# Layer-norm sums taken from nearly finished tiles, summed mLSTM strips, single-pass selector rows, three output units at the last heads, and four output transfers

## The reference: what is computed

```python
def layer_norm(x, g, b):
    xf = x.astype(jnp.float32)
    mu = jnp.mean(xf, axis=-1, keepdims=True)
    var = jnp.mean(jnp.square(xf - mu), axis=-1, keepdims=True)
    return ((xf - mu) * lax.rsqrt(var + LN_EPS)).astype(x.dtype) * g + b
...
    b = jnp.cumsum(lf, axis=-1)
    dmat = jnp.where(causal, b[..., :, None] - b[..., None, :] + ig[..., None, :], -jnp.inf)
...
    sm = w_intra * jnp.einsum('bhtd,bhsd->bhts', q, k)
    num = jnp.einsum('bhts,bhsv->bhtv', sm, v) + w_inter[..., None] * jnp.einsum('bhtd,bhdv->bhtv', q, C)
    den = jnp.sum(sm, axis=-1) + w_inter * jnp.einsum('bhtd,bhd->bht', q, n)
    h = num / jnp.maximum(jnp.abs(den), jnp.exp(-m_t))[..., None]
...
    h = h * lax.rsqrt(jnp.mean(h * h, axis=-1, keepdims=True) + RMS_EPS)
    return (h * jax.nn.sigmoid(o_pre)) @ w_out
```

## Time and profile before

| what | value |
|---|---|
| median of 3 runs | 2621.55 us (2618.34 to 2622.1) |
| the profiled execution | 2622.95 us |
| its span | 2620.9 us |
| outside the span | 2.05 us |
| PE busy | 95% of the span |
| granted TensorE clock, mean | 0.964 |

### The profile page before, as it was taken

The page is one execution under the profiler, slowest core; times in us unless marked ns, Lnnn a source line. Parts: engine busy times, 40 slices in busy tenths (PEclk is TensorE's granted clock), DMA queues, the critical chain, the costliest instruction groups (busy, mean ns, idle before and its releaser), DMA issues.

```text
span 2620.9 us, 33849 instructions
## 1 busy us (share of the span) xinstructions
PE 2480.9 (95%) x11937; PEld 2007.9 (77%) x11937; DVE 1488.6 (57%) x1796; ACT 499.2 (19%) x968; POOL 1647.5 (63%) x700
## 2 busy tenths in 40 slices
PE   6998999998999997999999999999999999999997
PEld 4776776776888875888888878888887667888886
DVE  5867324686464467755444465534688456544446
ACT  4533221103000004111111230000141442100000
POOL 4425544575777774756665657777777224787774
PEclk7999999998999997999999999999999888999998
DMA  6212333422332322222222223323322111232331
GB/s 241 74 54 85 114 148 128 157 73 66 96 104 86 102 87 67 85 77 77 83 78 84 77 76 96 109 77 98 108 82 81 41 33 49 92 104 84 96 106 54
DMA packets 61231, 237.72 MB, mean 91 GB/s; under 512 B 7072, under 2 KB 12200, under 8 KB 57424
## 3 DMA queue, kind: packets, MB, share of 16 engines
q1 hardware_dynamic: 54720, 230.51, 26.8%
q10 hardware_dynamic: 6416, 5.95, 0.7%
HBM read 232.24 MB, written 2.10 MB: 89 GB/s over the span
## 4 chain that ended last, share of the span: by engine, by line
PE 84%; DVE 8%; ACT 2%; issue 2%; DVEq 1%; ACTq 1%; DMA 1%; POOL 1%; POOLq 0%
PE gg L559 19%; PE gg L560 19%; PE gg L561 19%; PE babcd L597 2%; PE babcd L599 2%; PE babcd L598 2%; PE gg L934 2%; PE gg L936 1%; PE gg L935 1%; PE babcd L559 1%; PE babcd L560 1%; PE babcd L561 1%; PE babcd L1179 1%; PE be L910 1%; PE be L1205 1%
## 5 line engine op out<-in xcount | busy, mean ns | idle before, releaser
L467 POOL TENSOR_TENSOR w_hi<-raw,zero 128x1024 fp32r<-128x1024 f32 (+2 forms) x260 | 540.5, 2079 | 453.1 <-PE gg L561 348.2
L469 POOL TENSOR_TENSOR w_lo<-raw,w_hi 128x1024 fp32r<-128x1024 f32 (+2 forms) x260 | 695.3, 2674 | 37.7 <-issue 1.3
L559 PE MATMUL gg<-h_hi,w_hi 128*128 128x512 f32 x1560 | 621.0, 398 | 8.9 <-DVE bf L2349 4.9
L560 PE MATMUL gg<-h_lo,w_hi 128*128 128x512 f32 x1560 | 615.7, 395 | 0.0
L561 PE MATMUL gg<-h_hi,w_lo 128*128 128x512 f32 x1560 | 615.0, 394 | 0.0
L559 PEld LDWEIGHTS gg<-h_hi,w_hi 128*128 128x128 f32 x1560 | 298.2, 191 | 80.2 <-DVE bf L2349 7.2
L458 POOL TENSOR_TENSOR w_hi<-raw,zero 128x1024 fp32r<-128x1024 f32 (+2 forms) x64 | 139.8, 2184 | 332.1 <-PE babcd L561 153.7
L561 PEld LDWEIGHTS gg<-h_hi,w_lo 128*128 128x128 f32 x1560 | 297.8, 191 | 63.2
L560 PEld LDWEIGHTS gg<-h_lo,w_hi 128*128 128x128 f32 x1560 | 298.4, 191 | 61.3
L2059 DVE TENSOR_TENSOR ta<-ff_s,gg 128x512 f32<-128x512 f32 x63 | 43.4, 688 | 320.3 <-PE gg L561 320.3
L559 PE MATMUL gg<-u_hi,w_hi 128*128 128x512 f32 x528 | 209.7, 397 | 4.2 <-issue 4.2
(11 more groups left out here) (601 smaller groups left out, 3916.7 us busy)
## 6 DMA issues: line engine op xcount, KB each, us to landing
raw<-in_w_ff_in_a SPq DMA_DIRECT2D x66, 512.0 KB, 3.5
raw<-in_w_ff_in_b SPq DMA_DIRECT2D x66, 512.0 KB, 3.5
raw<-in_w_att_qk SPq DMA_DIRECT2D x48, 512.0 KB, 3.5
raw<-in_w_ff_out_a SPq DMA_DIRECT2D x24, 704.0 KB, 4.1
raw<-in_w_ff_out_b SPq DMA_DIRECT2D x24, 704.0 KB, 4.1
late_raw<-in_w_ada SPq DMA_DIRECT2D x16, 1024.0 KB, 5.0
raw<-in_w_ml SPq DMA_DIRECT2D x25, 512.0 KB, 3.5
raw<-in_w_merge_a SPq DMA_DIRECT2D x16, 768.0 KB, 5.6
```

The source lines that it names most:

```text
L467: pool.tensor_tensor(hi, a, zero[:].to_broadcast([P, size * P]), ALU.add)
L469: pool.tensor_tensor(lo, a, hi, ALU.subtract).then_inc(S["units_split"], 1)
L559: pe.matmul(dst, w_hi[slot][:, blk], xs[0][:, k, :], start=k == 0, stop=False)
L560: pe.matmul(dst, w_hi[slot][:, blk], xs[1][:, k, :], start=False, stop=False)
```

## The change

LN0 and LN1: tile 7 is no longer added to `ta` and `tb`. PE column-sums `ta` and `tb` of tiles 0 to 6 as soon as they are ready, then tile 7 and its square, and makes the row sums last, in two float32 matmuls. Centring and scaling are done tile by tile, and POOL makes `h_lo` (`low_tiles`), behind its third split. Attention: three blocks of unit 0 stand ahead of head 7's scores, and the third unit is done inside the last head, in a bank of its own. mLSTM projections: `gate_sums` moves from conv 3 to conv 1, `gate_columns` from conv 5 to conv 4, `gate_turn` from ahead of conv unit 7 to behind it; a new `gate_rows` after conv 2 splits the gate rows into rounded and rest parts (fp32r, partitions 0 to 7 and 32 to 39), so that a selector on 40 partitions spreads a row in a single pass. ACT loads that selector five times over and rounds it. Heads: the rows of head i+1 stand behind head i's values, score block 2 stands inside the gate unit after its fourth block, and the denominator takes two matmuls (128 and 384 wide) in place of four, from `sm_sum`, which DVE adds up in three instructions. `last_heads` takes the third output unit in. End: the last square is summed by PE alone, and four transfers of 512 KB from two queues, each as soon as its two tiles are ready.

```diff
+            def low_tiles(stage):
+
+                for k in range(KD):
+                    pool.wait_ge(S["h_high"], H_SPLIT[stage] - 7 + k)
+                    pool.tensor_tensor(h_lo[:, k, :], (ta, tb)[k % 2][:], h_hi[:, k, :], ALU.subtract).then_inc(S["h_split"], 1)
...
+                        if s == 2 and name in ("w_ff0_in_a", "w_att"):
+                            low_tiles("ff0" if name == "w_ff0_in_a" else "att")
...
                 pe.wait_ge(S["x_summed"], nth + 1)
-                pe.matmul(bf[:], ones[:], ta[:], start=True, stop=True).then_inc(S["ln_rows"], 1)
-                for n, a in enumerate((ta, tb)):
-                    for b in range(TB):
-                        mm = pe.matmul(be[:, n * TB + b:n * TB + b + 1], a[:, b * P:(b + 1) * P], ones[:, 0:1], start=True, stop=True)
-                mm.then_inc(S["ln_sum"], 1)
+                sums(0, ta, start=True)
+                sums(1, tb)
+                pe.wait_ge(S["ln_centred"], nth * 8 + 8)
+                sums(0, last)
+                pe.wait_ge(S["sq_ready"], (SQ["ln0"], SQ["ln1"])[nth] * 8 + 8)
+                sums(1, sq[1], stop=True).then_inc(S["ln_sum"], 1)
+                pe.matmul(bf[:], ones[:], ta[:], start=True, stop=False)
+                pe.matmul(bf[:], ones[:], last, start=False, stop=True).then_inc(S["ln_rows"], 1)
...
-                    for s in range(2):
+                    for s in range(int(lead is not None and isinstance(i, int)), 2):
...
-                        third = lead is not None and isinstance(i, int) and s == 0
-                        cols_mm(g[(u0 + s) % 2], THIRD[name] if third else (u0 + s) % 2, kb, xs, **(first if isinstance(i, int) and s == 0 else {}))
+                        cols_mm(g[(u0 + s) % 2], (u0 + s) % 2, kb, xs, **(first if isinstance(i, int) and s == 0 else {}))
...
+                    bank, slot = ((g[u0 % 2], u0 % 2), (g[(u0 + 1) % 2], (u0 + 1) % 2), (bf[:], THIRD["w_att_out"]))[s]
...
+                        tile_mm(bank, slot, k, (o_hi, o_lo))
                 pe.wait_ge(S["att_copied"], 48)
+                unit(0, 0, 3)
                 att_scores(7, 1)
-                unit(0, 0, 7)
+                unit(0, 3, 7)
                 att_swap(7)
                 unit(1, 0, 7)
                 att_turn(7)
+                unit(2, 0, 4)
                 att_values(7, 1)
-                unit(0, 7, 8)
-                unit(1, 7, 8)
+                unit(2, 4, 7)
+                for s in range(3):
+                    unit(s, 7, 8)
...
                     pe.wait_ge(S["ml_w"], i)
-                    pe.wait_ge(S["ml_sm"], 4 * i)
-                pe.matmul(ba if i else be[:], sel8[:, i, :], g_r[:], start=True, stop=True)
-                pe.matmul(bb if i else bf[:], sel8[:, i, :], g_m[:], start=True, stop=True).then_inc(S["ml_rows"], 1)
+                    pe.wait_ge(S["ml_sm"], 5 * i - 1)
+                pe.matmul(ba if i else be[:], sel[:, i, :], g_r2[:], start=True, stop=True)
+                pe.matmul(bb if i else bf[:], sel[:, i, :], g_m2[:], start=True, stop=True).then_inc(S["ml_rows"], 1)
...
-                wait(pe, "ml_sm", 4 * i)
+                wait(pe, "ml_sm", 5 * i)
                 if i == 0:
                     pe.wait_ge(S["conv_in"], 8)
-                for j in (0, 1, 3, 2):
-                    if j == 2:
+                def block(j):
+                    return pe.matmul(score_bank(i, j), ml_qk[rows, it + 4, j * P:(j + 1) * P], ml_qk[rows, it, j * P:SEQ],
+                                     start=True, stop=True)
+                for j in (0, 1, 3):
+                    block(j)
+                def third_block(k):
+                    if k == 4:
                         pe.wait_ge(S["ml_em"], i + 1)
-                    mm = pe.matmul(score_bank(i, j), ml_qk[rows, it + 4, j * P:(j + 1) * P], ml_qk[rows, it, j * P:SEQ],
-                                   start=True, stop=True)
-                mm.then_inc(S["ml_scores"], 1)
...
-                    pe.wait_ge(S["ml_sm"], 4 * i + j + 1 if i else 4)
+                    pe.wait_ge(S["ml_sm"], 5 * i + j + 1 if i else 4)
                     part = sm_t[:, ML_AT[j]:ML_AT[j] + SEQ - j * P]
                     pe.matmul(be[:, j * P:SEQ], ml_v[:, j, i * P:(i + 1) * P], part, start=j == 0, stop=j == 3)
-                    mm = pe.matmul(bf[:, j * P:SEQ], ones[:], part, start=j == 0, stop=j == 3)
-                mm.then_inc(S["ml_num"], 1)
+            def head_sums(i):
+
+                pe.wait_ge(S["ml_sm"], 5 * i + 5)
+                pe.matmul(bf[:, 0:P], ones[:], sm_t[:, 0:P], start=True, stop=True)
+                pe.matmul(bf[:, P:SEQ], ones[:], sm_sum[:], start=True, stop=True).then_inc(S["ml_num"], 1)
...
                 conv_unit(n)
+                if n == 7:
+                    gate_turn()
                 value_unit(n - 1)
                 if n == 2:
                     pe.wait_ge(S["gates_read"], 1)
                     inverse_columns(5, bf)
-                if n == 6:
-                    gate_turn()
             head_rows(0)
             value_unit(7)
             for i in range(8):
-                if i:
-                    head_rows(i)
-                head_scores(i)
-                output_gate(i)
+                output_gate(i, head_scores(i))
                 if i > 1:
                     norm_rows(i - 2)
                 head_values(i)
                 if i:
                     square_sums(i - 1)
+                if i < 7:
+                    head_rows(i + 1)
+                head_sums(i)
...
+                    bank, slot = ((g[u0 % 2], u0 % 2), (g[(u0 + 1) % 2], (u0 + 1) % 2), (be[:], THIRD["w_ml_out"]))[s]
+                    if first == 0:
+                        ready(u0 + s)
...
+                        tile_mm(bank, slot, k, (hd_hi, hd_lo), H_SPLIT["head"] - 8)
...
+                unit(2, 0, 2)
                 norm_rows(7)
+                unit(2, 2, 6)
                 for k in (6, 7):
-                    for s in range(2):
+                    for s in range(3):
                         unit(s, k, k + 1)
...
+            for a, name, value in ((tb, "sq_added", nth * 8 + 7), (sq[1], "sq_ready", nth * 8 + 8)):
+                pe.wait_ge(S[name], value)
+                for b in range(TB):
+                    mm = pe.matmul(be[:, b:b + 1], a[:, b * P:(b + 1) * P], ones[:, 0:1], start=a is tb and b == 0,
+                                   stop=a is not tb and b == TB - 1, skip_group_check=True)
+            mm.then_inc(S["sq_summed"], 1)
...
+            act.activation(sel[:], sel_in8[:], ACT.Copy)
...
+            for k in (0, 4):
+                act.wait_ge(S["out_ready"], k + 2)
+                act.dma_start(out[:, k:k + 2, :], x[:, k:k + 2, :]).then_inc(S["out_sent"], 16)
+            act.wait_ge(S["out_sent"], 64)
...
+                    third = {"w_att_out": bf[:], "w_ml_out": be[:]}.get(name)
+                    bank = third if third is not None and k == 2 else g[(u0 + s) % 2]
...
+                        if k == KD - 1:
+                            return
...
+                        if k == KD - 2:
+                            v.drain().then_inc(S["x_summed"], 1)
...
+                if squares != SQ["final"]:
+                    add_square(squares, KD - 1)
...
-                centre(4, KD)
-                v.drain()
-                wait(v, "rows_ready", nth + 1)
-                make(0)
-                make(1)
+                wait(v, "ln_rows", nth + 1)
                 for k in range(KD):
-                    wait(v, "h_high", H_SPLIT[stage] - 7 + k)
-                    v.tensor_tensor(h_lo[:, k, :], (ta, tb)[k % 2][:], h_hi[:, k, :], ALU.subtract).then_inc(S["h_split"], 1)
-                    if k + 2 < KD:
-                        make(k + 2)
+                    v.scalar_tensor_tensor(x[:, k, :], bf[:], -1.0 / D, x[:, k, :], ALU.mult, ALU.add)
+                    v.drain()
+                    if k == 0:
+                        wait(v, "rows_ready", nth + 1)
+                    make(k)
                 v.drain()
...
+            def gate_rows():
+                for whole_row, two in ((g_r, g_r2), (g_m, g_m2)):
+                    v.memset(two[:].bitcast(F32), 0.0)
+                    v.drain()
+                    v.tensor_copy(two[0:8, :], whole_row[:])
+                    v.drain()
+                    v.tensor_tensor(two[32:40, :], whole_row[:], two[0:8, :], ALU.subtract)
+                v.drain()
...
-                if n == 3:
+                if n == 1:
                     gate_sums()
-                if n == 5:
+                if n == 2:
+                    gate_rows()
+                if n == 4:
                     gate_columns()
...
+                v.drain()
+                own = lambda j: sm_t[:, ML_AT[j]:ML_AT[j] + SEQ - j * P]
+                tt(sm_sum[:], own(0)[:, P:SEQ], own(1), ALU.add)
+                tt(sm_sum[:, P:3 * P], sm_sum[:, P:3 * P], own(2), ALU.add)
```

(2 more changed lines are left out.)

73 lines of the change are left out of this document (40 added, 33 removed).

## The result

The changed kernel takes 2615.78 us (median of 13 runs, 2610.35 to 2619.85) against 2620.48 of the kernel before on the same chips (13 runs, 2615.69 to 2624.63): a ratio of 0.998, 95% interval 0.9971 to 0.999. It is faster by 4.7 us, which is near what can be told from no change, and not by the 49 that were forecast. The profiled execution has a span of 2616.8 us.

The account below looks back on a forecast made before the run. PE, busy 95% of the span, was taken as the bound; terms of −9.8 −0.4 −8.2 −25.8 −2.3 −2.6 = −49.1 us gave a span of 2571.8 and a median of 2572.5, range 2564 to 2582 (chance 0.50).

Parts of the forecast that it names:

- The loop that is: mLSTM heads: PE no longer bounds; a chain over additions, `og`, tanh, |den| and products takes 15.4 us a head.
- a clock above 0.9 in the heads: Sign to look for in the changed kernel's profile: PE's granted clock in the mLSTM heads, 0.84 before.
- 1.1 us a head: mLSTM heads: the first addition waits for the end of POOL's second split instruction, +1.1 us in each head.
- Rival (d): mLSTM heads: each of three additions waits for a whole POOL instruction, up to 7 us a head; chance 0.02.
- Rival (a): mLSTM heads: the clock falls as often as before, about 9 to 12 us more, 2583; chance 0.20.
- a loop of 13.2 on DVE and ACT: mLSTM heads: the forecast's sum for one head's chain without the three additions, 13.2 us.
- its 25.8: mLSTM heads: the gain forecast for seven heads, 103.3 us against 129.1.
- Layer norms: LN0 and LN1: additions gone and tiles scaled sooner, gains of 4.6 and 5.2 us, together −9.8.
- the case that I had named for −14: LN0 and LN1: outer bound of the gain, if the clock stays up through the sums.
- Third units: Last heads: filling PE's gaps gives −0.4 us in attention, −2.3 in mLSTM, as POOL's next split holds PE up.
- Projections: mLSTM projections: earlier gate work and single-pass rows gain, `gate_rows` costs PE 2.1 us; together −8.2 us.
- End: Kernel end: column sums replace the last add, +0.25 us; four 512 KB transfers, 3.5 us each, save 2.8; together −2.6.

Follow-up runs that it names:

- low_last: Changed kernel with `hd_lo` moved on DVE behind `og` and the two products of `head_norm`; 2604.86 us, ratio 0.9943.
- old_order_sums: old_heads with the strip additions and two denominator matmuls put back, right behind the value matmuls; 2594.51 us, ratio 0.9905.
- old_heads: four_strips with rows at a head's start and score block 2 ahead of the gate unit, as before the change; 2591.16 us, ratio 0.989.
- pool_waits: Changed kernel with POOL's split in the heads, and for the first two `w_ml_out` units, waiting for the gate copy; 2595.25 us, ratio 0.9902.
- sums_first: Changed kernel with denominator ahead of square sums and rows, `hd_lo` behind `og` and `head_norm`, POOL's split waiting for the `og` copy; 2586.36 us, ratio 0.9878.
- four_strips: Changed kernel without the strip additions, the denominator in four matmuls again; 2578.72 us, ratio 0.985.

## Why the prediction was wrong

**The step that failed** is the sum of "The loop that is" for the heads: 15.4 us a head, 103.3 for seven; measured are 19.6 and 137.4. That is 34 of the 45 us by which the span is off (2571.8 against 2616.8). The sum lacks a path and has a wait too small, and the clock, which it takes as high, fell with them. The loops, from windows of each trace:

| run | loop | PE idle in it | mean clock |
|---|---|---|---|
| before | 129.4 | 0.0 | 0.84 |
| changed kernel | 137.4 | 11.6 | 0.78 |
| low_last | 130.8 | 15.2 | 0.86 |
| old_order_sums | 126.9 | 14.5 | 0.81 |
| old_heads | 119.2 | 8.3 | 0.90 |
| pool_waits | 118.7 | 10.3 | 0.91 |
| sums_first | 105.6 | 9.0 | 0.98 |
| four_strips | 103.5 | 0.3 | 0.98 |

A mean clock of 0.78 over 137.4 us is some 30 us lost, in pool_waits at 0.91 some 11, so most of what was paid was paid at the lower clock and not in the waits themselves. The forecast asked for a clock above 0.9 in the heads.

First, the path. I let the loop run over `og`, tanh and |den|, with the denominator's matmuls free to go when the additions were done. But they stand on PE behind the square sums and the next rows, and the square sums wait for `og` (`og_copied`, in `square_sums`), which stands on DVE behind the additions and `hd_lo`. So the additions and this order of PE delay everything on it. pool_waits shows this without waits for POOL: its loop is 15.2 us longer than that of four_strips, about 2 in a plain cycle (16.96 against 14.73 to 15.0) and most of it in the two that have half clock. Of the 15.2, sums_first takes back 13.1 with the additions kept, by the denominator ahead of the square sums and `hd_lo` behind `og`, which were not tried apart. It is the order that cost, more than the additions themselves.

Second, place and size of the waits for POOL. I had 1.1 us a head, for the first addition, behind a split that starts ahead of the products. In the changed kernel the split starts behind the first addition in seven of eight heads, and the wait was up to 2.0 for the second, 2.0 for the third and 2.1 for `hd_lo`, in a queue behind which PE waits. The four waits of 2.8 to 3.2 us on PE were followed by half clock. Together 18.7 us of the loop (pool_waits). Rival (d), additions that wait out a whole instruction of POOL, came true for two in a head, in the changed kernel (at 2105.96), in low_last and in old_order_sums. I had held that the third finds POOL idle, and gave the rival 0.02; all waits for POOL together took 2.7 us a head. Rival (a) held for the half clock (mean 0.78, before 0.84), and its price was too low, since the slack that I set against it was not there. It comes with the waits: pool_waits has 0.91 and four_strips 1.00 in six of seven cycles.

The forecast's own terms also speak against the additions. Without them it has a loop of 13.2 on DVE and ACT, and on PE 15.5 less 1.45 for the rows, about 14.1: less than the 15.4 with them. four_strips measured 14.8 on the mean.

**Right in mechanism**: rows in a single pass, 1.46 a head (forecast 1.45, the agreement partly luck as said at old_heads). Rows and block 2 moved, 15.7 us with the clock it saves, which the forecast had within its 25.8; with four strips the loop is 103.5. The additions, which the forecast counted as 1.3 us won on PE in each head, make 34 us in the order of the changed kernel (137.4 against 103.5), 2.1 in that of sums_first, where POOL's split waits besides.

**Layer norms**: −12.4 against −9.8. LN0 gained 7.0 (forecast 4.6): the clock stayed full through its column sums and the first wide one (1.10, not 2.07), the case that I had named for −14. In LN1 it did not (2.05), and the gain was 5.4 (forecast 5.2).

**Third units**: the split of the fourth unit was named as what bounds them, rightly (4.17 us of waiting in both places). Left out was the half clock after that wait, 1.6 and 2.3 us. The −0.4 and −2.3 together measure +3.0; taken out of four_strips, the third units give 6.2 us back by the traces.

**Projections**: −5.2 against −8.2. `gate_rows` took 7.8 us (7 forecast), of which 4.05 reached PE, not 2. The second wait is that of a value bank: ACT's copy of it is queued behind the conv tile that is late, which I had not followed.

**Attention heads**: I let them cancel. They took 3.9 us more, for which see the last section, and 2.9 more ahead of them. Of the 2.9, some 2.2 are clock: PE is busy at half clock for 16.2 us there, before for 11.7. What brought that was not tried.

**End**: −3.4 against −2.6; a transfer took 2.7 us, not 3.5, and less than the 3.1 that the prediction worked out beside it. The section of the Trainium skill that it used for this ("DMA: Bandwidth & Descriptors", "Anatomy of one DMA — SWDGE (gpsimd) path") is on transfers issued from GpSimd; these come from SP and ACT.

## What to carry to other kernels

Before an operation is put on an engine's list, name what stands behind it in that list and who waits for that; its own length is the smaller part of its price. The three additions took 1.3 us of matmuls from PE; in an order where their result stands behind other waits they cost 4.8 a head, and in sums_first, where PE uses it at once and POOL's split waits, 0.3. And where units are handed on through few slots, filling one gap moves the wait to the next split, and the clock may fall on it.
